# A two-layer transformer trunk in fp32 on one Trainium2 core: reordered norm tails, late rows and last heads

## The reference, cut to what matters

```python
# T=512 tokens, D=1024, layer 0: dilated attention, layer 1: differential attention
for l in range(2):
    shift, scale, gate = ada_mod(c_act, mod_mix_w[l], mod_mix_b[l], 3)
    if l == 1:
        k_sh, v_sh = shared_kv(x, c_act, kv_norm, kv_mod_w, kv_mod_b, b_w_k, b_w_v, cos, sin)
    h = rms_norm(x, norm_pre_mix[l]) * (1.0 + scale) + shift
    y = dilated_mixer(h, a_w_qkv[l], a_w_o[l], cos, sin) if l == 0 else diff_mixer(h, k_sh, v_sh, ...)
    x = x + gate * rms_norm(y, norm_post_mix[l])
    shift, scale, gate = ada_mod(c_act, mod_ffn_w[l], mod_ffn_b[l], 3)
    h = rms_norm(x, norm_pre_ffn[l]) * (1.0 + scale) + shift
    y = conv_ffn(h, ffn_w_gate[l], ffn_w_up[l], ffn_conv_w[l], ffn_conv_b[l], ffn_w_down[l])
    x = x + gate * rms_norm(y, norm_post_ffn[l])
```

## Time and profile before

| | |
|---|---|
| median of 3 runs | 1463.88 us (1463.5 to 1464.41) |
| profiled execution | 1462.9 us, its span 1461.1 us |
| PE busy | 1409.7 us, 96% of the span |
| DVE, ACT, POOL busy | 888.3, 589.3, 146.9 us |
| mean granted clock of PE | 0.987 |

### The profile page before, as it was taken

How to read it: one execution, slowest core, us unless ns; L and a number is a source line. 1 busy time by engine, 2 the same in 40 slices (tenths; PEclk the granted TensorE clock), 3 DMA queues, 4 the chain that set the end, 5 groups by cost and what they waited for, 6 DMA issues and landing times.

```text
span 1461.1 us, 18237 instructions
## 1 busy us (share of the span) xinstructions
PE 1409.7 (96%) x7096; PEld 1154.7 (79%) x7096; DVE 888.3 (61%) x1571; ACT 589.3 (40%) x1019; POOL 146.9 (10%) x250
## 2 busy tenths in 40 slices
PE   4999999999999999999999999998999999999998
PEld 3789888888698788887886787776888878887886
DVE  7777877764468777773556438887357544443223
ACT  4533444445543334332215426776444333332112
POOL 2002100000211111110112001222121000000000
PEclk9999999999999999999999899999999999999999
DMA  9437433321046655553651221212126333232331
GB/s 333 142 93 224 145 102 116 97 92 30 29 146 201 184 163 184 182 164 98 205 186 45 87 72 58 59 59 72 44 78 184 99 92 96 87 101 87 101 89 70
DMA packets 168668, 171.51 MB, mean 117 GB/s; under 512 B 5269, under 2 KB 140806, under 8 KB 168582
## 3 DMA queue, kind: packets, MB, share of 16 engines
q1 hardware_dynamic: 154224, 119.59, 27.0%
q0 software_dynamic: 13824, 50.34, 10.6%
q10 hardware_dynamic: 534, 0.41, 0.1%
HBM read 168.22 MB, written 2.10 MB: 117 GB/s over the span
## 4 chain that ended last, share of the span: by engine, by line
PE 82%; DVE 8%; ACT 4%; issue 3%; POOL 2%; DMA 1%; SPq 0%; ACTq 0%; DVEq 0%; POOLq 0%
PE ps L624 19%; PE ps L552 15%; PE ps L554 15%; PE ps L553 15%; PE ps L1076 3%; PE ps L783 3%; PE ps L890 3%; PE ps L854 2%; ACT prob L1689 2%; PE ps L606 1%; PE ps L595 1%; DVE prob L2340 1%; PE ps L1193 1%; PE ps L911 1%; PE ps L674 1%
## 5 line engine op out<-in xcount | busy, mean ns | idle before, releaser
L552 PE MATMUL ps<-hhi,whi 128*128 128x512 f32 (+1 forms) x1008 | 396.7, 394 | 5.2 <-DVE hlo L1876 4.6
L1801 DVE TENSOR_TENSOR wlo<-raw,whi 128x1024 fp32r<-128x1024 f32 x200 | 244.0, 1221 | 241.7 <-ACT whi L1299 241.6
L554 PE MATMUL ps<-hhi,wlo 128*128 128x512 f32 (+1 forms) x1008 | 388.6, 386 | 0.0
L553 PE MATMUL ps<-hlo,whi 128*128 128x512 f32 (+1 forms) x1008 | 388.1, 385 | 0.0
L1299 ACT ACTIVATE whi<-raw 128x1024 fp32r<-128x1024 f32 x200 | 210.1, 1052 | 258.2 <-PE ps L624 175.7
L552 PEld LDWEIGHTS ps<-hhi,whi 128*128 128x128 f32 x1008 | 190.0, 188 | 46.7 <-issue 6.4
L554 PEld LDWEIGHTS ps<-hhi,wlo 128*128 128x128 f32 x1008 | 189.9, 188 | 41.6
L553 PEld LDWEIGHTS ps<-hlo,whi 128*128 128x128 f32 x1008 | 190.3, 189 | 39.3 <-issue 1.0
L1926 DVE SCALAR_TENSOR_TENSOR macc<-mraw,csil,macc 128x256 f32<-128x256 f32 x294 | 142.2, 484 | 14.1 <-DMA mraw<-in_mod_ffn_w_dram 5.0
L624 PE MATMUL ps<-whi,ghi 128*128 128x512 f32 x352 | 110.7, 395 | 1.7 <-DVE tmp L2279 1.7
L624 PE MATMUL ps<-wlo,ghi 128*128 128x512 f32 x352 | 110.9, 396 | 0.0
(11 more groups left out here) (276 smaller groups left out, 2046.7 us busy)
## 6 DMA issues: line engine op xcount, KB each, us to landing
mraw<-in_mod_ffn_w_dram POOLq DMA_DIRECT2D x48, 512.0 KB, 4.0
raw<-in_ffn_w_gate_dram SPq DMA_DIRECT2D x44, 512.0 KB, 3.8
raw<-in_ffn_w_up_dram SPq DMA_DIRECT2D x44, 512.0 KB, 3.7
raw<-in_ffn_w_down_dram SPq DMA_DIRECT2D x44, 512.0 KB, 3.6
mraw<-in_mod_mix_w_dram POOLq DMA_DIRECT2D x32, 512.0 KB, 3.9
raw<-in_a_w_qkv_dram SPq DMA_DIRECT2D x28, 512.0 KB, 4.0
mstart<-in_mod_mix_w_dram SPq DMA_DIRECT2D x8, 1024.0 KB, 14.6
mraw<-in_kv_mod_w_dram POOLq DMA_DIRECT2D x16, 512.0 KB, 3.8
```

The costliest lines, as they stand in the source:

```text
L552: pe.matmul(out_, whi[:, slot, cols], rhs_hi, start=first, stop=False)
L553: pe.matmul(out_, whi[:, slot, cols], rhs_lo, start=False, stop=False)
L554: return pe.matmul(out_, wlo[:, slot, cols], rhs_hi, start=False, stop=last)
L1801: dve.tensor_tensor(wlo[:, slot, :], raw[:, slot, :], head, ALU.subtract).then_inc(*at.here(lo_ready, ahead))
```

## The change

In words: (1) in all three normed tails the norm of the first token pair stands ahead of tile 3's squares, in A and F also ahead of the second half of tile 2's work (`added(2)`), in B (`last_apart`) tile 2's work comes after the norm as well. (2) `turn_x(0)` and `turn_x(1)` stand earlier among PE's last products. (3) Stage F keeps a fourth row for the end, split into free memory of `ghi`, `glo` (`SPARE`). (4) `WARM` is 8 instead of 24. (5) The values of the first tile of the last pair are halved around the first scores; the head of the first turned output waits for the last scores. (6) Splits and `lead_of_b` of heads 6 and 7 are reordered, and row 7 has its own memory (`row7`). (7) `values_chunk(0, 0)` and `(0, 2)` run row by row and wait for one row at a time, and DVE makes the whole copy for row 0. Buffers move where memory must be free longer.

```diff
-    WARM, WARM_START, WARM_SUMS = 24, 8, 12
+    WARM, WARM_START, WARM_SUMS = 8, 8, 12
...
@@ PE: token_stage
-                for k in range(kt - 3):
+                rows = 4 if norms else 3
+                for k in range(kt - rows):
...
                 for t in range(NT):
-                    for b in range(3):
+                    for b in range(rows):
                         if t == 0:
-                            operands(kt - 3 + b, b)
-                        mm = token_products(hi, lo, slots[b], t, kt - 3 + b, kt == 3 and b == 0, b == 2)
+                            operands(kt - rows + b, b)
+                        if norms and t == NT - 1 and b < 2:
+                            turn_x(b)
+                        mm = row_products(hi, lo, *last_rows[b], t, kt - rows + b, False, b == rows - 1)
...
@@ PE: values_chunk
+                if g == 0 and c in (0, 2):
+                    for k in (2 * c, 2 * c + 1):
+                        pe.wait_ge(*at.done(h_ready, k))
...
@@ PE: attend_pair, last pair
-                    last_values(0)
+                    last_values(0, range(4))
                     scores_pair(0)
+                    last_values(0, range(4, DT))
                     scores_pair(1)
@@ PE: output_of_a
                 for k in range(2 if early == 3 else 0, 3):
+                    if k == 2:
+                        turn_x(0)
                     mm = products(3, k)
...
-                turn_x(0)
+                turn_x(1)
                 products(3, 3).then_inc(*at.here(chunk_used, 3))
                 at.passed("chunk", PAIRS)
-                turn_x(1)
@@ PE: fill
                     if quarter == 2:
                         pe.wait_ge(*at.done(pair_free, -2))
-                        lead_of_b(0, 0, range(4))
+                    lead_of_b(0, 0, (0, 1) if quarter == 2 else (2,))
                 elif quarter == 0:
                     pe.wait_ge(*at.done(pair_free, -1))
-                    lead_of_b(0, 1, range(4))
+                    lead_of_b(0, 1, range(3))
+                    for half in range(2):
+                        lead_of_b(0, half, (3,))
@@ PE: output_of_b
                 for k in range(HEADS_B):
+                    if k in (4, 6):
+                        turn_x(k // 2 - 2)
                     mm = products(2, k)
...
@@ ACT: token_stage
                     square_y(1)
-                    square_y(2)
                     square_x(1)
-                    split_next()
-                    square_y(3)
-                    square_x(2)
+                    if not last_apart:
+                        square_y(2)
                     for n, norm in enumerate(norms):
                         fronts(0, norm, n)
                     heads(0, norms[0])
-                    square_x(3)
+                    if last_apart:
+                        square_y(2)
+                        square_x(2)
+                    split_next()
+                    square_y(3)
+                    if not last_apart:
+                        square_x(2)
+                    split_next()
                     for norm in norms[1:]:
                         heads(0, norm)
-                    split_next()
+                    square_x(3)
                     split_next()
@@ DVE: token_stage
+                    if k == kt - 4 and norms:
+                        dve.wait_ge(*at.done(hi_ready, 2))
+                        dve.tensor_tensor(SPARE[1], raw[:, (at.n["chunk"] + 2) % 3, :], SPARE[0].bitcast(F32),
+                                          ALU.subtract).then_inc(*at.here(lo_ready, 2))
+                    else:
+                        split_rest()
...
-                    gained(2)
-                    added(2)
-                    split_next()
-                    gained(3)
+                    if not last_apart:
+                        gained(2)
                     for n, norm in enumerate(norms):
                         backs(0, norm, n)
+                    rests(0, norms[0])
+                    if last_apart:
+                        gained(2)
+                        added(2)
+                    split_next()
+                    if not last_apart:
+                        added(2)
+                    gained(3)
                     added(3)
-                    for norm in norms:
+                    split_next()
+                    for norm in norms[1:]:
                         rests(0, norm)
-                    split_next()
                     split_next()
@@ ACT, heads of layer 1 (DVE alike)
-                if head < HEADS_B - 1:
+                if head < HEADS_B - 2:
                     chunk()
+                exp_b(head, 3)
                 if head == HEADS_B - 2:
-                    split_row(3)
-                exp_b(head, 3)
+                    chunk()
```

More of the change, by code:

```diff
@@ L153, in yoco_trunk @@
             qk_odd = [sb(name, [P, T], F32R, odd_mem) for name in ("qhi2", "qlo2", "khi2", "klo2")]
+        with ExitStack() as odd_mem:
+            row7 = [sb(name, [P, D], F32R, odd_mem) for name in ("row7_hi", "row7_lo")]
         mraw = sb("mraw", [P, 2, DT // 2, 2 * P])
@@ L405, in row_of_b @@
                 return whi[:, slots[k], :], wlo[:, slots[k], :]
-            a, j = ((khi, klo), 2 * (k - 3)) if k < 7 else ((hhi, hlo), 0)
-            return tuple(part[:, j:j + 2, :].rearrange("p a n -> p (a n)") for part in a)
+            if k == 7:
+                return row7[0][:], row7[1][:]
+            return tuple(part[:, 2 * (k - 3):2 * (k - 3) + 2, :].rearrange("p a n -> p (a n)") for part in (khi, klo))
+        SPARE = [part[:, FT - 6:FT - 4, :].rearrange("p a n -> p (a n)") for part in (ghi, glo)]
         def value_cols(g):
@@ L720, in token_stage @@
                         at.passed("ydone")
-                at.passed("chunk", 3)
+                at.passed("chunk", rows)
                 if norms:
-                    turn_x(1)
                     pe.wait_ge(*at.done(u_ready, 2))
@@ L769, in values_chunk @@
                 pe.wait_ge(*at.done(lo_ready))
+                slot = at.at("chunk", 3)
+                if g == 0 and c in (0, 2):
+                    for k in (2 * c, 2 * c + 1):
+                        pe.wait_ge(*at.done(h_ready, k))
+                        w = slice(k % 2 * value_cols(g), (k % 2 + 1) * value_cols(g))
+                        for t in range(NT):
+                            for n, (a, b) in enumerate(((hhi, whi), (hhi, wlo), (hlo, whi))):
+                                mm = pe.matmul(ps[:, t, 0:value_cols(g)], a[:, k, tile_cols(t)], b[:, slot, w], start=(k == 0 and n == 0), stop=False)
+                    mm.then_inc(*at.here(chunk_used))
+                    at.passed("chunk")
+                    return
                 if g == 0:
                     pe.wait_ge(*at.done(h_ready, 2 * c + 1))
-                slot = at.at("chunk", 3)
                 for t in range(NT):
@@ L898, in turn_o, with last_values @@
                     at.passed("ojob")
-                def last_values(p):
+                def last_values(p, ks=range(DT)):
                     if p:
@@ L904, in last_values @@
                     else:
-                        pe.wait_ge(*at.done(lo_ready))
-                        pe.wait_ge(*at.done(lo_ready, 1))
-                    for k in range(DT):
+                        pe.wait_ge(*at.done(lo_ready, ks[0] // 4))
+                        pe.wait_ge(*at.done(lo_ready, ks[-1] // 4))
+                    for k in ks:
                         slot = (at.n["chunk"] + k // 4) % 3
@@ L1314, in junk, with token_stage @@
                 return tmp[:, 2 * j:2 * j + 2, :].rearrange("p a n -> p (a n)")
-            def token_stage(kt, buffers, norms, diags=False, split_ahead=0):
+            def token_stage(kt, buffers, norms, split_ahead=0, last_apart=False):
                 full = buffers[1]
-                if diags:
-                    spread_gain(0)
-                    spread_gain(1)
                 for k in range(split_ahead, kt - 3):
                     at.passed("chunk")
-                    split_head()
+                    if k == kt - 4 and norms:
+                        act.wait_ge(*at.done(w_landed, 2))
+                        act.wait_ge(*at.done(chunk_used, -2))
+                        act.activation(SPARE[0], raw[:, (at.n["chunk"] + 2) % 3, :], ACT.Copy).then_inc(*at.here(hi_ready, 2))
+                    else:
+                        split_head()
                 split = [0]
@@ L1747, in _ @@
                     chunk()
+                else:
+                    split_row(5)
                 read_turned_b(head, 0)
@@ L1825, in split_last_row_of_a, with token_stage @@
                                   ALU.subtract).then_inc(*at.here(lo_ready, 2))
-            def token_stage(kt, buffers, norms, late=None, split_ahead=0):
+            def token_stage(kt, buffers, norms, late=None, split_ahead=0, last_apart=False):
                 u, full = buffers
@@ L1831, in token_stage @@
```

(7 more changed lines are left out.)

54 lines of the change are left out of this document (26 added, 28 removed).

## The result

The changed kernel took 1465.62 us (median of 20 runs, 1462.68 to 1470.5), the kernel before beside it on the same chip 1464.3 (20 runs, 1458.47 to 1465.62). The ratio of their times is 1.0021, 95% interval 1.0013 to 1.0029, so +3.1 us (1.9 to 4.2): a little slower, and inside the stated range. The profiled execution took 1467.09 us, its span 1465.3, 4.2 more than before.

What follows compares the result with a forecast made beforehand. The prediction took PE, busy 96% of the span, to bound the kernel. Its terms 0 - 1.4 + 3.4 + 4.0 - 0.9 - 3.5 = +1.6 on 1463.9 gave 1465.5 us, range 1457 to 1470.

Steps and rivals of the forecast that it cites:

- The start, 0: First chunks of values: waiting row by row gains nothing where both rows are there; 0 us.
- The last pair, -1.4: Layer 0's last pair: 12 halved matmuls fill 1.4 of PE's 2.04 us wait for maxima; bounds 0 and -4.8.
- A, +3.4: End of stage A: entry 1.2 us earlier, but tiles 2 and 3 late, so +3.4 us; bounds +2.5 and +4.0.
- POOL needs 1.6 after it: Step in A: after the square of tile 3's x is read, POOL takes 1.6 us to the matrix, at 410.5.
- F, +4.0: End of stage F: fourth row's wait 1.6 us, tile 3 late, its turn at half clock; +4.0 us, bounds -0.4 and +5.
- POOL beside VectorE: In F, POOL's three operations beside DVE's splits and rests were taken as 4.4 us, against 1.6 in A.
- Heads, -0.9: Heads 6 and 7, layer 1: -1.76 - 1.2 + 1.2 + 0.9 = -0.9 us; bounds -2.7 and +2.
- B, -3.5: End of stage B: PE begins 4.6 us earlier, the second pair then limits; -3.5 us, bounds -4.6 and -1.5.
- The clock rival: Norm tails: with 8 useless matmuls instead of 24 the clock falls; one more half-clock stretch, +3.4, so 1469 us; chance 0.20.
- The sign of being wrong: Wrong if A and F enter earlier than 1.2 and 2.5 us without second-pair turn waits, or unnamed 0.50 stretches appear.
- The rival of vanished stretches: Half-clock stretches at 350.15 and 800.7 go, one net of what was booked: -3.4 to -6, about 1460 us; chance 0.17.
- Tiles 2 and 3 not late: In A and F the turns do not wait for tiles 2 and 3: -11.9, about 1452 us; chance 0.11.

Runs made afterwards that it cites:

- pair_only: The kernel before with only the halved values of layer 0's last pair, the later head of the first turned output and the moved buffers: 0.9989 of the kernel before.
- heads_new: pair_and_b with the changed order of heads 6 and 7 of layer 1: 0.9967 of the kernel before.
- pair_and_b: The kernel before with only the last pair's halved values (later head of first turned output), stage B's changed tail and the moved buffers: 0.9959 of the kernel before.
- heads_old: The changed kernel with heads 6 and 7 of layer 1 ordered as in the kernel before: 1.0017 of the kernel before.
- warm24: The changed kernel with 24 useless matmuls again instead of 8: 1.0042 of the kernel before.
- added2_warm: added2_first with 24, 20 and 8 useless matmuls in A, F and B: 0.998 of the kernel before.
- added2_first: The changed kernel with tile 2's addition (and its square) ahead of the first norm's backs in A and F: 0.9981 of the kernel before.

## Why the prediction was right, and where not

The forecast was 1465.5 with +1.6 us; measured 1465.62, and +3.1 (1.9 to 4.2) by the ratio. The agreement of the medians is partly luck: they lie 1.3 us apart, the means of the 20 runs 2.9, and the ratio says 3.1. The terms owe less to luck.

- **The start, 0**: right; the means are 104.7 in both codes.
- **The last pair, -1.4**: as forecast, -1.4 by the profiles (the old code was profiled once, and the new lies between 286.2 and 289.4) and -1.6 by pair_only (-3.5 to +0.3). Firm is only that the wait fell from 2.04 to 0.41. Of the stretch at 350 half went, but new ones came at 202 and 263: the half clock between the first two rows was 10.2 us in both profiles.
- **A, +3.4**: +4.3 by the profiles, above the upper bound of 4.0. Entry at 401.13 (forecast 401.1), tile 3's turn forecast to end at 412.4, measured 413.4. The step that was too small: "POOL needs 1.6 after it" took 2.7 (square read by 408.6, matrix at 411.27), since its last operation ran beside a split.
- **F, +4.0**: +4.1 by the means, +3.5 at equal half clock. Less A's lag of 4.3, the trace follows the chain closely: the wait for the fourth row, put at 1.6, was 1.46; entry 799.25 (forecast 799.1); tile 3's addition starts at 804.2 (804.3); POOL is done at 810.55 (811.3); the turn, at half clock as forecast, ends at 814.5 (814.8); the second pair's product starts at 821.65 (822.1). In this one pair of profiles only +1.9 stood behind F, since the stretch at 834.8 was half as long after the change, which other profiles of the old code had too.
- **POOL beside VectorE** was the sum's largest duration without a good row. POOL's three operations in F took 1.08 (at 811.09), 1.40 and 1.10, that is 0.86, 0.83 and 0.48 more than the 0.22, 0.57 and 0.62 they take alone. The Trainium skill ("SBUF — State Buffer", section "SBUF: two separate sides") has them wait for a whole VectorE operation in progress: each excess lies under the 1.22 us of a split, as the rule would have it, and so does the 1.0 of POOL's last operation in A. The 2.15 of the earlier trace rows, 1.5 over, is more than one split explains. I had read that one row against the rule; these four speak for it.
- **Heads, -0.9**: wrong in sign, +1.6 by the means and +0.9 at equal half clock, inside the bounds. By the times it is +1.2 (heads_new against pair_and_b) and +0.6 (changed against heads_old), neither clear of noise. The step "of the 2.56 at 1008.37 about 1.2 goes" failed: three waits of 7.4 us took the place of three of 5.0. The split that PE awaits (3.56) was seen; the transposes that wait for the join behind the rotation (2.28) were not counted as a wait of their own, and 6.8 to 13.7 us at half clock stood there, against 3.4 or 6.8 with the old order.
- **B, -3.5**: right, -3.5, with one wait of 1.38 at tile 3 as forecast.
- **The clock rival** (0.20): the stretch that it named did appear at 400.1, and at the entry of A it is not the cause: with that entry at full clock tile 3's turn comes no earlier (warm24: 19.04 against 19.05 us), and added2_warm gained nothing. For the whole kernel the rival stays open in part. The changed kernel's 20 executions have 49 us at half clock in the mean; the 89 of the kernel before that were timed beside the three later rounds have 39 (those of the result itself have no clock on record), and there the span rises by about 0.35 us for each us more at half clock (correlation 0.91). At that price ten more us would be the whole +3.1; at the 0.15 that the changed kernel's own executions show (correlation 0.44) they would be half of it.
- **What comes ahead of a stretch**: the prediction read that stretches at 0.50 follow weak ones, and that each is a little under 7 us. Those at 800.7 and 1008.9 do follow weak ones, but in the 3.4 us ahead of those at 350.15 and 834.8 in the same trace PE was busy for all 3.40, and the one at 319.4 is 3.4 long.
- **The sign of being wrong** that the prediction gave itself, half-clock stretches in places that it had not named, came true: 48.5, 202.1, 263.5 and 1017.9 (where the kernel before has one at 1008.9). The number held in spite of it.
- **The rival of vanished stretches**: they moved by chance. **Tiles 2 and 3 not late**: false for this change; added2_first made it half true and won 5.9 us.

The terms now sum to 0 - 1.4 + 4.3 + 4.1 + 1.6 - 3.5 = +5.1, two above the +3.1 of the times; the spread of a stage between profiles of the same code (up to 4.4 us in F) is enough for that, but it isn't settled. What is shown is that the place of tile 2's work in A and F costs more than the change loses; how the +3.1 divides between the order and the clock is not.

What beats both kernels by most is **pair_and_b**, 0.9959 of the kernel before.

## What to carry to other kernels

When a norm is moved ahead of other tiles' work, follow the last tile to its end too: the entry came 1.2 us earlier and the second half 4 later, and tile 2's addition (with its square) put back ahead of the norm won 5.9. Reorderings on two engines can need each other, so undoing one half tests the half, not the change. And a stretch at half clock cost nothing where PE would have waited anyway (added2_warm, A), but 1.6 us where it fell on the turn that the stage waits for (warm24): look whether the work under it is due, and compare stages at equal half clock.

## What the runs showed that was not expected

- The same code of a stage differs between profiled executions by 1.6 us in A (113.5 to 115.1) and 4.4 in F (228.2 to 232.6), in step with the half clock that fell there, while the stretches from 506 to 666 and behind 1331 repeat within 0.1; single profiles can't price a term of 2 us in such a stage.
- Half-clock stretches of 3.4 us turned up inside dense work (48.5, 202 and 263 us in the changed kernel's trace, between 258 and 264 in twelve of the fourteen), with PE busy for all of the 3.40 us ahead of those at 48.5 and 263.5, in runs of matmuls of 1 and 64 columns. The fourteen profiles lasted 1454.6 to 1468.4 us with 32 to 55 us at half clock. Between kernels the total does not tell the time (added2_first had 51 at 1458.0 us, warm24 43 at 1466.0); between the 89 executions of the kernel before it goes with the time (correlation 0.91, above).
- Moving the turns ahead of a stage's last product needs the norm ahead of tile 3: with that order alone undone the entry waited 7.0 (A) and 7.8 us (F). The turns alone were not undone.
